# Gate and up tiles of the second block's feed-forward parts as seven half-size products, down tiles dealt out behind them

## The chip, the cores and the metric

The kernel runs on one core of a Trainium2 chip, as one launch. The metric is the device time of that launch in microseconds, the median of three runs. TensorE does the matrix products, VectorE and ScalarE the elementwise work, SyncE (SP) and GpSimd (POOL) issue the DMAs. SBUF is the on-chip memory, PSUM the banks in which TensorE accumulates.

## The reference, cut to what matters

Two blocks of two layers each work on one sequence of 512 tokens and 1024 features, in float32. What the change touches is the second block's feed-forward, which each of its two layers has twice (before and after its mixer), so four times in all:

```python
def swiglu_2(h, w_gu, w_down):
    g, u = jnp.split(h @ w_gu, 2, axis=-1)
    return (jax.nn.silu(g) * u) @ w_down

for l in range(DEPTH):
    h = modulate(rms_norm_2(x, ffn1_norm[l]), mod[0], mod[1])
    x = x + FFN_RESIDUAL * (1 + mod[2])[:, None, :] * swiglu_2(h, ffn1_w_gu[l], ffn1_w_down[l])
    ...
    h = modulate(rms_norm_2(x, ffn2_norm[l]), mod[6], mod[7])
    x = x + FFN_RESIDUAL * (1 + mod[8])[:, None, :] * swiglu_2(h, ffn2_w_gu[l], ffn2_w_down[l])
```

Here h is 512 x 1024, w_gu 1024 x 5632 and w_down 2816 x 1024, and DEPTH is 2. The hidden width of 2816 is 22 tiles of 128 for the gate and 22 for up.

## The kernel before, in words

**Layout and format.** Features lie on the 128 partitions, tokens along the free axis: `xT` is the residual stream, eight slices (KT = 8) of 128 features by 512 tokens. Every matrix product is made of three: a float32 operand z is split into a rounded part `_hi` and the rest `_lo`, both in the fp32r format, and the product is w_hi·h_hi + w_lo·h_hi + w_hi·h_lo. `highs` (L1124) issues the first two (L1127, L1128), `lows` (L1130) the third (L1132). Weights are the stationary operand, 128 by 128, activations the moving one, 512 columns. A gate or up tile (128 hidden features) takes 8 slices x 3 = 24 matmuls.

**A weight tile's way.** SyncE's `load` (L522) fetches 512 KB into one of three places of `raw` once the place is free; ScalarE's `hi` (L674) rounds it into `w_hi` (L678), VectorE's `lo_of` (L1737) writes raw - w_hi into `w_lo` (L1740) and frees the place. TensorE's `tile` (L1141) waits in `slot_ready` for `w_lo` and for the PSUM place of `psP` (three places also) and runs the matmuls. ScalarE's `evac` (L680) copies the bank to `ybuf` (L684). With each tile that it empties, ScalarE rounds the weights of the tile three further on, and VectorE splits them behind its own work on the tile emptied: this order is written out by hand on every engine, and each engine's queue is strictly in order.

**A feed-forward part.** `PARTS` cuts the 22 pairs of gate and up into 8, 7 and 7. For each group, `ffn` runs the pairs, then all 8 down tiles over this group's hidden slices (3 matmuls for each slice), and adds them to `xT`. After a pair VectorE's `gated` (L1859) multiplies SiLU(gate) by up (L1866) and splits the product into `a_hi` (L1869) and `a_lo` (L1870). Each down tile is emptied by ScalarE with the layer's gate as scale, and added by VectorE in `residual` (L1840, add at L1855); with the last group, VectorE also squares and sums `xT` for the next norm (`squares`, L1767), and the eighth tile is added in two halves straight from PSUM (L1851).

**The norm ahead of a part.** TensorE sums the squares over the partitions, VectorE finds the factor (`root`), TensorE spreads it, and VectorE's `scaled` (L1808) writes each slice times gain into one of two places of `tb` (L1824), ScalarE adds the shift and rounds into `h_hi` (L734), VectorE writes `h_lo` (L1818). TensorE starts on the first two tiles (`two_tiles`) as soon as the first slice is there.

**Engines.** SyncE issues all of these loads. POOL has nothing to do in the second block but seven small copies in each layer (L663). The parts are F2 (before the mixer) and F3 (after it), for l = 0 and 1.

## Time and profile before

| | |
|---|---|
| median of 3 runs | 3531.23 us (3527.92 to 3532.91) |
| span of the profiled execution, first to last instruction | 3529.6 us |
| instructions | 45935 |
| TensorE busy | 3498.3 us, 99%, 17160 matmuls |
| VectorE busy | 2067.0 us, 59% |
| ScalarE busy | 1307.9 us, 37% |
| DMA | 387.35 MB, mean 110 GB/s |

The span comes from one profiled execution, and lies 1.6 us below the median of the timed runs. In the rows below, a group reads: line, engine, operation, output <- inputs by name, shapes, how often | busy us, mean ns of one | idle us of the engine just before, and what ended it. PE is TensorE's matmuls, PEld its weight loads, DVE VectorE, ACT ScalarE. A stage's row gives its length, then for PE, PEld, DVE, ACT and POOL the busy time with the number of instructions, then the granted TensorE clock (1.00 is full speed), the share of time the DMA engines were busy, and GB/s. A row in order of time gives start and length in us; "x8" is eight of the same merged.

### The profile page before, as it was taken

To read this page: it belongs to the slowest core of one execution; us is meant where nothing else is said; L and a number is where in the kernel's file an instruction comes from. 1 tells how busy PE (TensorE), PEld (TensorE's weight loads), DVE (VectorE), ACT (ScalarE), POOL (GpSimd) and SP (SyncE) were. 2 spreads that over 40 slices of the span, in tenths; PEclk is the share of its full clock that TensorE was granted. 3 is DMA by queue.
4 is the path that set the end of the run, shared out by engine and by line. 5 is a ranking of instruction groups with operands and counts; after the bars stand their busy time and mean duration, and the time that the engine had idled before them with its cause. 6 is when DMAs were issued, how large, how long until landed. Compare 5 with 4: busy or idle time off the path is not lost.

```text
span 3529.6 us, 45935 instructions
## 1 busy us (share of the span) xinstructions
PE 3498.3 (99%) x17160; PEld 2837.1 (80%) x17160; DVE 2067.0 (59%) x3447; ACT 1307.9 (37%) x2145; POOL 63.8 (2%) x122
## 2 busy tenths in 40 slices
PE   9999999999999999999999999999999999999999
PEld 7777777888876788888888887888888887878887
DVE  5777776666876566685334767433443347673334
ACT  5555554222343332333323444323332234442222
POOL 0000000000000000000000000000000000000000
PEclk9999999999999999999999999999999999999999
DMA  4222223656421365652232212323323322223232
GB/s 145 85 65 78 76 65 106 216 200 206 168 71 49 108 200 194 206 187 94 96 95 93 80 66 73 103 99 96 95 90 97 99 91 77 72 73 100 94 101 79
DMA packets 142102, 387.35 MB, mean 110 GB/s; under 512 B 21680, under 2 KB 63024, under 8 KB 141936
## 3 DMA queue, kind: packets, MB, share of 16 engines
q1 hardware_dynamic: 127024, 306.65, 27.1%
q0 software_dynamic: 14912, 78.52, 6.5%
q8 instruction: 100, 1.64, 0.2%
q14 instruction: 66, 0.54, 0.0%
HBM read 382.11 MB, written 2.10 MB: 109 GB/s over the span
## 4 chain that ended last, share of the span: by engine, by line
PE 95%; DVE 3%; issue 1%; ACT 1%; DMA 0%; SPq 0%; DVEq 0%; ACTq 0%
PE psP L1127 26%; PE psP L1132 25%; PE psP L1128 25%; PE psP L1278 3%; PE psP L1285 3%; PE psP L1279 3%; PE psS L1624 1%; PE psM L1647 1%; PE psS L1341 1%; PE psS L1507 1%; PE psS L1310 1%; PE psS L1323 0%; PE psS L1491 0%; PE psS L1329 0%; PE psS L1635 0%
## 5 line engine op out<-in xcount | busy, mean ns | idle before, releaser
L1127 PE MATMUL psP<-h_hi,w_hi 128*128 128x512 f32 x2664 | 1052.5, 395 | 4.8 <-ACT h_hi L734 2.3
L1128 PE MATMUL psP<-h_hi,w_lo 128*128 128x512 f32 x2664 | 1037.7, 390 | 0.0
L1132 PE MATMUL psP<-h_lo,w_hi 128*128 128x512 f32 x2664 | 1027.8, 390 | 0.0
L1740 DVE TENSOR_TENSOR w_lo<-raw,w_hi 128x1024 fp32r<-128x1024 f32 (+1 forms) x456 | 546.7, 1199 | 396.5 <-ACT w_hi L678 390.4
L684 ACT ACTIVATE ybuf<-psP 128x512 f32<-128x512 f32 (+1 forms) x401 | 239.4, 597 | 1199.5 <-PE psP L1132 1198.1
L1127 PEld LDWEIGHTS psP<-h_hi,w_hi 128*128 128x128 f32 x2664 | 500.5, 188 | 127.2 <-issue 25.8
L1132 PEld LDWEIGHTS psP<-h_lo,w_hi 128*128 128x128 f32 x2664 | 498.3, 188 | 107.7 <-DVE h_lo L1818 4.2
L1128 PEld LDWEIGHTS psP<-h_hi,w_lo 128*128 128x128 f32 x2664 | 500.8, 188 | 99.4
L678 ACT ACTIVATE w_hi<-raw 128x1024 fp32r<-128x1024 f32 (+1 forms) x456 | 471.0, 1033 | 65.4 <-PE psP L1132 65.4
L1127 PE MATMUL psP<-a_hi,w_hi 128*128 128x512 f32 x1248 | 486.3, 390 | 1.2 <-ACT a_hi L1080 1.2
L1128 PE MATMUL psP<-a_hi,w_lo 128*128 128x512 f32 x1248 | 485.6, 389 | 0.0
L1132 PE MATMUL psP<-a_lo,w_hi 128*128 128x512 f32 x1248 | 482.1, 390 | 0.0
L1866 DVE TENSOR_TENSOR prod<-ybuf 128x512 f32<-128x512 f32 x132 | 91.3, 692 | 390.0 <-ACT ybuf L684 343.2
L1855 DVE TENSOR_TENSOR xT<-xT,ybuf 128x512 f32<-128x512 f32 x166 | 114.5, 690 | 279.5 <-ACT ybuf L684 279.5
L1127 PEld LDWEIGHTS psP<-a_hi,w_hi 128*128 128x128 f32 x1248 | 234.2, 188 | 52.3 <-ACT a_hi L1080 2.0
L1132 PEld LDWEIGHTS psP<-a_lo,w_hi 128*128 128x128 f32 x1248 | 233.9, 188 | 49.1 <-DVE a_lo L2521 0.9
L1128 PEld LDWEIGHTS psP<-a_hi,w_lo 128*128 128x128 f32 x1248 | 234.3, 188 | 48.1
L684 ACT ACTIVATE ybuf<-psP,gate 128x512 f32<-128x512 f32 x106 | 72.9, 688 | 314.7 <-PE psP L1132 314.7
L1931 DVE SCALAR_TENSOR_TENSOR ada_acc<-adaw,cact,ada_acc 128x1536 f32<-128x1536 f32 x84 | 152.4, 1814 | 3.4
L1278 PE MATMUL psP<-w_more_hi,a_hi 128*128 128x512 f32 x264 | 109.4, 414 | 0.0
L1285 PE MATMUL psP<-w_more_hi,a_lo 128*128 128x512 f32 x264 | 104.5, 396 | 0.0
L1279 PE MATMUL psP<-w_more_lo,a_hi 128*128 128x512 f32 x264 | 104.4, 395 | 0.0
(336 smaller groups left out, 3545.9 us busy)
## 6 DMA issues: line engine op xcount, KB each, us to landing
raw<-in_gu SPq DMA_DIRECT2D x264, 512.0 KB, 3.3
adaw<-in_ada POOLq DMA_DIRECT2D x96, 768.0 KB, 5.7
raw<-in_down SPq DMA_DIRECT2D x96, 448.0 KB, 3.3
raw<-in_down SPq DMA_DIRECT2D x48, 512.0 KB, 3.6
raw<-in_qkv SPq DMA_DIRECT2D x40, 512.0 KB, 3.6
raw<-in_mix_in SPq DMA_DIRECT2D x34, 512.0 KB, 3.2
raw<-in_qkv SPq DMA_DIRECT2D x64, 256.0 KB, 3.1
raw<-in_wo SPq DMA_DIRECT2D x32, 512.0 KB, 3.3
```

The costliest lines, as they stand in the source:

```text
L678: nc.scalar.activation(w_hi[:, s, 0:cols], raw[:, s, 0:cols], copy).then_inc(hi_done, 1)
L684: nc.scalar.activation(ybuf[0:m, s, :], psP[0:m, s, :], func, **kw).then_inc(evac_done, 1)
L1127: nc.tensor.matmul(psP[:, s, :], hi, rhs[0](kt), start=(n == 0), stop=False)
L1128: nc.tensor.matmul(psP[:, s, :], lo, rhs[0](kt), start=False, stop=False)
L1132: mm = nc.tensor.matmul(psP[:, s, :], w_hi[:, s, kt * P:kt * P + P], rhs[1](kt), start=False, stop=(n == K - 1))
L1278: nc.tensor.matmul(psP[:, m % RING, :], tokens, hi, start=(kt == 0), stop=False)
L1279: nc.tensor.matmul(psP[:, m % RING, :], tokens, lo, start=False, stop=False)
L1285: mm = nc.tensor.matmul(psP[:, m % RING, :], src[1](kt)[:, r * P:(r + 1) * P], hi, start=False, stop=(kt == KT - 1))
L1740: v.tensor_tensor(w_lo[:, s, 0:cols], raw[:, s, 0:cols], w_hi[:, s, 0:cols].bitcast(F32), ALU.subtract)\
L1855: used(v.tensor_tensor(xT[:, m, :], xT[:, m, :], y(), ALU.add), wait=N is not None)
L1866: used(v.tensor_tensor(prod[:, :], g, up, ALU.mult), 2)
L1931: i = v.scalar_tensor_tensor(total, w, at, total, ALU.mult, ALU.add)
```

## The change

All of it lies in F2 and F3. The other parts of the kernel are as before.

- Three of the 22 pairs stay plain tiles. For the other 19, the pair is seen as one product of 2 x 2 blocks: gate and up by the two halves of the 1024 features (weights, blocks of 128 x 512), and the two halves of the features by the early and the late 256 tokens. `product` forms it as seven products of block sums (Winograd's form of Strassen's scheme), each 4 slices x 3 matmuls of 256 columns, in the order P1, P5, P6, P3, P7, P2, P4, accumulated in three PSUM banks (A, E, B).
- Sums of tokens: four combinations of the normed slices (`token_sums`), once for each part, split into `ht_hi` and `ht_lo` (`token_highs` on ScalarE, `token_lows` on VectorE), ahead of and between the first two plain pairs. For them the norm keeps its unshifted slices (`normed_at`) in place of the two places of `tb`.
- Sums of weights, for each pair: SyncE loads five blocks of 256 KB into `s_raw` (A11, S1, S3, A12, A22, with A22 in A11's place), POOL adds a second block onto S1 and onto S3 with an accumulating DMA (`weight_sums`), VectorE forms S2 = A11 + S1 and S4 = A12 + S2. ScalarE rounds and VectorE splits them in four groups (G2: S2, S4; G1: A11, S1; G3: S3, A12; G4: A22).
- Between the products ScalarE copies bank A or E to `st_c` (after P1, P5, P6, P7); TensorE waits for such a copy before it goes on in the same bank. VectorE joins the parts, ScalarE takes SiLU, VectorE gates, ScalarE writes `a_hi`, VectorE `a_lo`.
- Down tiles: six groups of pairs (3, 4, 4, 4, 3, 4) in place of three. A group's eight down tiles are dealt out behind the pairs of the next group, two behind each (3, 3, 2 where that group has three), and the last group's eight stand at the end. VectorE adds each straight from PSUM with the gate (`added`); ScalarE no longer empties them.

```diff
+SEVEN_PARTS = ((0, 3), (3, 4), (7, 4), (11, 4), (15, 3), (18, 4))
+PRODUCTS = (("A", A11, "b11"), ("E", S1, "t1"), ("A", S2, "t2"), ("E", S4, "b22"), ("A", S3, "t3"), ("B", A12, "b21"), ("A", A22, "t4"))
...
@@ sync: ffn_seven @@
+                def load_s1(q):
+                    if q < PAIRS:
+                        if F.pair(l, q):
+                            sp.wait_ge(*s_low.at(low(q - 1, G1)))
+                        sp.dma_start(s_raw[:, S1, :], up_of(q)[:, 0:T]).then_inc(s_landed["s1"].sem, 16)
...
+                for q, (_, _, tiles) in enumerate(frames):
+                    load_a11(q + 1)
+                    load_a22(q + 1)
+                    load_s1(q + 2)
+                    down_load()
+                    load_s3_a12(q + 2)
+                    for _ in tiles[1:]:
+                        down_load()
...
@@ gpsimd: weight_sums @@
+                for q in range(PAIRS):
+                    tile = l * 2 * FT + 2 * (PLAIN + q)
+                    pool.wait_ge(*s_landed["s1"].at(16 * (F.pair(l, q) + 1)))
+                    pool.dma_start(s_raw[:, S1, :], F.gu[tile + 1][:, T:2 * T], accum_op=ALU.add).then_inc(s1_added.sem, 16)
+                    pool.wait_ge(*s_landed["s3"].at(16 * (F.pair(l, q) + 1)))
+                    pool.dma_start(s_raw[:, S3, :], F.gu[tile][:, 0:T], accum_op=ALU.add).then_inc(s3_added.sem, 16)
...
@@ scalar: ffn_seven, for each pair @@
+                    copied(q, P1, "A", C1)
+                    highs_4(q)
+                    copied(q, P5, "E", C5)
+                    copied(q, P6, "A", C2)
+                    copied(q, P7, "A", C3)
+                    if more:
+                        highs_2(q + 1)
+                    act.wait_ge(*s_joined.at(3 * F.pair(l, q) + 3))
+                    nc.scalar.activation(st_c[:, q % 2, C1:C1 + 2, :], st_c[:, q % 2, C1:C1 + 2, :], ACT.Silu).then_inc(s_silu.sem, 1)
+                    if more:
+                        highs_1(q + 1)
+                    act.wait_ge(*s_gated.at(2 * F.pair(l, q) + 2))
...
+                    if more:
+                        highs_3(q + 1)
+                    for _ in tiles:
+                        pos.step()
+                        ahead()
...
@@ tensor: ffn_seven @@
+                def product(p):
+                    name, slot, src = PRODUCTS[p - 1]
+                    fresh = p in (P1, P5, P2)
+                    for k in range(HK):
+                        hi, lo = s_hi[:, slot, k * P:k * P + P], s_lo[:, slot, k * P:k * P + P]
+                        high, low = moving[src](h_hi, ht_hi, k), moving[src](h_lo, ht_lo, k)
+                        start, stop = fresh and k == 0, k == HK - 1
+                        nc.tensor.matmul(bank[name], hi, high, start=start, stop=False, skip_group_check=True)
+                        nc.tensor.matmul(bank[name], lo, high, start=False, stop=False, skip_group_check=True)
+                        mm = nc.tensor.matmul(bank[name], hi, low, start=False, stop=stop, skip_group_check=True)
+                    mm.then_inc(s_product.sem, 1)
...
+                    pe.wait_ge(*s_low.at(4 * pair + G1))
+                    if q:
+                        pe.wait_ge(*s_gated.at(2 * pair))
+                    product(P1)
+                    if q == 0:
+                        pe.wait_ge(t_low, 2 * HK * (F.turn(l) + 1))
+                    product(P5)
+                    pe.wait_ge(*s_copied.at(4 * pair + 1))
+                    product(P6)
+                    pe.wait_ge(*s_copied.at(4 * pair + 2))
+                    product(P3)
+                    pe.wait_ge(*s_low.at(4 * pair + G3))
+                    pe.wait_ge(*s_copied.at(4 * pair + 3))
+                    product(P7)
+                    product(P2)
+                    pe.wait_ge(*s_low.at(4 * pair + G4))
+                    pe.wait_ge(*s_copied.at(4 * pair + 4))
+                    product(P4)
+                    for d, m in tiles:
...
+                        down(d)
...
@@ vector: ffn_seven @@
+                token_sums(0)
+                token_sums(1)
+                token_lows(0)
+                token_lows(1)
+                plain_pair(0)
+                token_sums(2)
+                token_sums(3)
+                token_lows(2)
+                token_lows(3)
+                plain_pair(1)
+                sum_2(0)
+                sum_4(0)
+                lows(0, G2, S2, 2)
+                lows(0, G1, A11, 2)
+                lows(0, G3, S3, 2)
+                plain_pair(2)
+                for q, (n, f, tiles) in enumerate(frames):
+                    more = q + 1 < PAIRS
+                    lows(q, G4, A22, 1)
+                    gate_late(q)
+                    if more:
+                        sum_2(q + 1)
+                    up_late(q)
+                    if more:
+                        sum_4(q + 1)
+                    gate_early(q)
+                    if more:
+                        lows(q + 1, G2, S2, 2)
+                    activated(q)
+                    if more:
+                        lows(q + 1, G1, A11, 2)
+                    a_low(q, n, f)
+                    if more:
+                        lows(q + 1, G3, S3, 2)
+                    for _, m in tiles:
+                        added(m)
+                        ahead()
```

Here `sum_2` and `sum_4` wait for the landings and for POOL's sum on S1, `gate_late` for P3, `up_late` for the copy of P7, `gate_early` for P2, `activated` for the SiLU and for P4; each `highs_n` of ScalarE waits for its inputs and for the product that last read its place; `ahead` prepares the weights of the down tile three further on.

## Rows read from the trace of the kernel before

**Rows 1.** The page: its first line, and busy time by engine.

```profile
span 3529.6 us, 45935 instructions
PE 3498.3 (99%) x17160; PEld 2837.1 (80%) x17160; DVE 2067.0 (59%) x3447; ACT 1307.9 (37%) x2145; POOL 63.8 (2%) x122
```

**Rows 2.** The page's chain that ended last, by engine.

```profile
PE 95%; DVE 3%; issue 1%; ACT 1%; DMA 0%; SPq 0%; DVEq 0%; ACTq 0%
```

**Rows 3.** By stage: block 2's first part, then one of block 1.

```profile
1600.20:1959.20 359.00, 359.00 (x1586) 296.54 (x1584) 154.46 (x199) 112.53 (x144) 0.00 (x0) 1.00 0.30 95
...
600.00:962.00 362.00, 361.41 (x1596) 298.76 (x1597) 256.38 (x261) 111.17 (x146) 24.40 (x45) 1.00 0.59 201
```

**Rows 4.** Costliest groups within 1600.2 to 1959.2 us, each shape by itself.

```profile
L1127 PE MATMUL psP<-h_hi,w_hi 128*128 128x512 f32 x351 | 136.6, 389 | 0.0
...
L1127 PEld LDWEIGHTS psP<-h_hi,w_hi 128*128 128x128 f32 x350 | 65.7, 188 | 13.8
...
L1740 DVE TENSOR_TENSOR w_lo<-raw,w_hi 128x1024 fp32r<-128x1024 f32 x53 | 64.9, 1225 | 65.4 <-ACT w_hi L678 65.4
L678 ACT ACTIVATE w_hi<-raw 128x1024 fp32r<-128x1024 f32 x53 | 55.8, 1052 | 0.0
...
L684 ACT ACTIVATE ybuf<-psP 128x512 f32<-128x512 f32 x44 | 26.3, 599 | 155.8 <-PE psP L1132 155.7
...
L1870 DVE TENSOR_TENSOR a_lo<-prod,a_hi 128x512 f32 x18 | 12.5, 692 | 2.7 <-DVE a_hi L1869 0.7
L1869 DVE CAST a_hi<-prod 128x512 f32 x18 | 7.6, 420 | 0.0
```

**Rows 5.** Short matmuls: order of time (start, length), then one stretch.

```profile
1003.91 1.05 PE L1472 MATMUL psS<-qd,kd 128*128 128x128 f32 x8
1004.80 0.27 PE L1477 MATMUL psS<-ident,ke 128*128 128x128 f32 x1
...
1025.12 0.19 PEld L1127 LDWEIGHTS psP<-h_hi,w_hi 128*128 128x128 f32 x1 [0.38 <-issue]
1025.23 0.19 PEld L1128 LDWEIGHTS psP<-h_hi,w_lo 128*128 128x128 f32 x1
...
543.05:552.80 9.75, 9.66 (x122) 6.60 (x120) 5.54 (x22) 4.39 (x11) 0.00 (x0) 1.00 0.17 55
```

**Rows 6.** Groups of the whole span: shapes nearest to the new ones.

```profile
L1824 DVE SCALAR_TENSOR_TENSOR tb<-xT,gs,psS 128x512 f32<-128x512 f32 x48 | 35.4, 747 | 5.6 <-PE psS L1194 4.0
...
L2229 DVE SCALAR_TENSOR_TENSOR state<-state,decay,psS 128x256 f32<-128x256 f32 x48 | 20.8, 475 | 10.5 <-PE psS L1491 10.5
...
L2063 DVE TENSOR_TENSOR rot<-rot,rot 128x256 f32<-128x256 f32 x32 | 13.6, 425 | 1.1
...
L2362 DVE TENSOR_TENSOR w_lo<-raw,w_hi 128x384 fp32r<-128x384 f32 x16 | 8.9, 555 | 0.2
...
L844 ACT ACTIVATE qk<-psS 128x256 f32<-128x256 f32 x32 | 12.1, 380 | 18.9 <-PE psS L1310 18.9
```

**Rows 7.** DMA issues: size, and median us from issue to landing.

```profile
raw<-in_gu SPq DMA_DIRECT2D x264, 512.0 KB, 3.3
adaw<-in_ada POOLq DMA_DIRECT2D x96, 768.0 KB, 5.7
...
raw<-in_uq SPq DMA_DIRECT2D x16, 192.0 KB, 2.3
...
xT<-in_x POOLq DMA_DIRECT2D x8, 256.0 KB, 3.0
```

**Rows 8.** In order of time: the first part's beginning, TensorE, then VectorE.

```profile
1599.45 0.47 PE L1127 MATMUL psP<-h_hi,w_hi 128*128 128x512 f32 x1 [0.61 <-ACT h_hi L734]
...
1609.56 0.68 DVE L1747 TENSOR_TENSOR w_lo<-raw,w_hi 128x512 fp32r<-128x512 f32 x1
```

**Rows 9.** In order of time: the first part's end, VectorE.

```profile
1957.17 1.22 DVE L1740 TENSOR_TENSOR w_lo<-raw,w_hi 128x1024 fp32r<-128x1024 f32 x1
...
1959.14 0.88 DVE L1851 SCALAR_TENSOR_TENSOR xT<-psP,gate,xT 128x256 f32<-128x256 f32 x2 [0.75 <-PE psP L1132]
```

More of the change, by code:

```diff
@@ L33 @@
 PARTS = ((0, 8), (8, 7), (15, 7))
+SEVEN_PARTS = ((0, 3), (3, 4), (7, 4), (11, 4), (15, 3), (18, 4))
+PLAIN = SEVEN_PARTS[0][1]
+PAIRS = FT - PLAIN
+HK, HT = 4, T // 2
+A11, S1, S2, S4, S3, A12 = range(6)
+A22 = A11
+PRODUCTS = (("A", A11, "b11"), ("E", S1, "t1"), ("A", S2, "t2"), ("E", S4, "b22"), ("A", S3, "t3"), ("B", A12, "b21"), ("A", A22, "t4"))
+P1, P5, P6, P3, P7, P2, P4 = range(1, 8)
+G2, G1, G3, G4 = range(1, 5)
+C1, C2, C3, C5 = 0, 1, 2, 3
 RING = 3
@@ L87, in kt_of, with seven_frames, a_place @@
     return 3 if kind == "q" else KT
+def seven_frames():
+    frames = []
+    for n, (f0, nf) in enumerate(SEVEN_PARTS[1:]):
+        for j in range(nf):
+            first, end = -(-KT * j // nf), -(-KT * (j + 1) // nf)
+            frames.append((n + 1, f0 + j, [(n, m) for m in range(first, end)]))
+    return frames
+def a_place(n):
+    return n % 2 * HK
 def step_units(n):
@@ L458, in __init__, with turn, pair @@
                 self.a_ready = sem(name + "_a_ready")
+            def turn(self, l):
+                return 2 * l + (1 if self is F3 else 0)
+            def pair(self, l, q):
+                return self.turn(l) * PAIRS + q
         ada_landed = [sem(f"ada_landed{i}") for i in range(ADA_RING)]
@@ L723, in hi_half, with norm @@
                     i.then_inc(hi_done, 1)
[L725 removed]
+            def norm(N, l, dst, sh=None, kept=None):
                 hi_half(0)
@@ L1239, in ffn, with ffn_seven, down @@
                             tile(nf, a_split, before=a_wait if m == 0 else None, beside=beside)
+            def ffn_seven(F, l):
+                bank = {"A": psS[:, 0, T:T + HT], "E": psS[:, 1, 0:HT], "B": psS[:, 1, T:T + HT]}
+                early, late = slice(0, HT), slice(HT, T)
+                moving = {"b11": lambda z, t, k: z[:, k, early], "b21": lambda z, t, k: z[:, HK + k, early],
+                          "b22": lambda z, t, k: z[:, HK + k, late], "t1": lambda z, t, k: t[:, k, 0, :],
+                          "t3": lambda z, t, k: t[:, k, 1, :], "t2": lambda z, t, k: t[:, k, 2, :], "t4": lambda z, t, k: t[:, k, 3, :]}
+                def product(p):
[9 more added lines that the diff above has]
+                    mm.then_inc(s_product.sem, 1)
+                def down(n):
+                    nf, at = SEVEN_PARTS[n][1], a_place(n)
+                    tile(nf, ((lambda kt: a_hi[:, at + kt, :]), (lambda kt: a_lo[:, at + kt, :])))
+                two_tiles(KT, h_split, h_wait(F.norm, l))
+                for _ in range(2 * PLAIN - 2):
+                    tile(KT, h_split)
+                a_waited = -1
+                for q, (n, f, tiles) in enumerate(seven_frames()):
+                    pair = F.pair(l, q)
+                    pe.wait_ge(*s_low.at(4 * pair + G1))
+                    if q:
+                        pe.wait_ge(*s_gated.at(2 * pair))
[15 more added lines that the diff above has]
+                    for d, m in tiles:
+                        if d > a_waited:
+                            pe.wait_ge(F.a_ready, l * FT + sum(SEVEN_PARTS[d]) + 1)
+                            a_waited = d
+                        down(d)
+                pe.wait_ge(F.a_ready, l * FT + FT + 1)
+                for m in range(KT):
+                    down(len(SEVEN_PARTS) - 1)
```

270 lines of the change are left out of this document (249 added, 21 removed).

## The prediction

> **What bounds the kernel now.** I read the page's busy times first: TensorE is busy for 99% of the span, VectorE 59%, ScalarE 37% [rows 1]. The chain that ended last says the same from the other side, 95% of it is TensorE [rows 2]. The table by stage then shows the four feed-forward parts of the second block, each a stretch of 359.0 us in which TensorE never stops: 1584 matmuls of 512 columns (44 gate and up tiles of 24, then 8 down tiles of 66), at a granted clock of 1.00 and with DMA at 0.30 of its time or less [rows 3] (the first stretch stands there; the other three have 359.0 too). 359.0 / 1584 = 0.2266 us from one matmul to the next. The single rows give 0.389 us to a matmul and 0.188 us to its weight load [rows 4]; they overlap, so neither is a price. The spacing is. Everything else in these stretches has room: what counts is the number of matmuls, the spacing of each kind, and what can make TensorE wait.
>
> **What the change does to TensorE.** Three of 22 pairs stay plain: 6 x 24 = 144 matmuls, 144 x 0.2266 = 32.6 us. The other 19 pairs went through 48 matmuls of 512 columns, 10.88 us. They become seven products of 4 x 3 = 12 matmuls, 84 of 256 columns. In columns that is 21504 for 24576, one eighth less; in matmuls it is 36 more, and each brings a weight load of its own. Down stays 528 matmuls, 119.6 us, only cut into 48 tiles in place of 24.
>
> So the spacing s of a 256-column matmul with its own 128-column load decides, and the trace has none in this number format. The bounds: [rows 5] show eight 128-column matmuls of full fp32, each with a 128-column load of its own, in 0.89 us, 0.111 each: loads can follow each other that closely while short matmuls run. Where a stretch begins, the second load starts 0.11 after the first [rows 5], so 0.11 is also what a load of our format holds the array up. Half of today's spacing is 0.113. The granted clock of 1.00 is the 2.4 GHz level, where 512 columns are 0.2133 us; if the 0.0133 above that belongs to each matmul and not to each column, s = 0.1067 + 0.0133 = 0.120. The far end is 0.188, a weight load's whole length. I take **0.117**, between 0.113 and 0.120, which are the rows of the same format. Then 19 x 84 x 0.117 = 186.7 us for 206.7: a part falls from 359.0 to 338.9, and four parts save 80 us.
>
> A rule gives more. The Trainium skill, "TensorE: Matmul & The Clock Gate", section "Back-to-back issue gap", puts a warm matmul's gap at its columns over 2.4 GHz plus 2.5 ns. By it s would be 0.109, estimated from that page, and the sum some 50 us lower. The trace disagrees at 512 columns, where it shows 0.2266 and the page says about 0.216.
>
> **Issue.** 84 loads and 84 matmuls in 9.8 us are one instruction per 0.058 us. The densest stretch of the attention ran 122 matmuls and 120 loads in 9.75 us, 0.040 each [rows 5], so issue does not bind at 0.117.
>
> **VectorE at the head of each part.** Its queue is in order. Today TensorE begins at 1599.45 and VectorE ends the norm at 1610.24, 10.8 us later [rows 8]; after it there is slack. Now the four token sums and their splits come first: per slice one add of 0.425, three of 0.475, two splits of 0.69 [rows 4, 6], 3.2 us, 13.0 for four. Two gated pairs with four weight splits add 7.9, the two weight sums 1.4, two splits of two planes 2.5. A gated pair is 0.69 for the product, 0.42 and 0.69 for its two parts [rows 4]. That is 24.8, so 35.6 after the beginning; one wait for ScalarE's rounding (1.05 [rows 4]) and some 20 links of 0.07 make it 38.1. TensorE has only 32.6 us of plain tiles. It loses **5.5 us** a part, the first 2 to 3 of them before tile 3, whose weight split now stands behind the sums; 22 us in all. The lower end is nothing, if the queue packs better; the upper is 8 a part.
>
> **VectorE at the tail.** The last eight down tiles have 12 matmuls, 2.72 us each, where they had 21 (4.76). VectorE has to add the tile (0.75 [rows 6]), square, add (0.69 each) and split the next weights (0.69, or 1.23 for the last three), 2.9 to 3.4 us. Today it ends its last split and then idles 0.75 us before the final residual [rows 9], which follows TensorE's last matmul. Now it falls behind by 0.2 to 0.7 a tile, from a start behind TensorE (the last pair's a_lo is done only 2.6 us after P4), and reaches that residual about 2.2 us late. Three parts have weights to prepare there: **6.6 us**. Before, ScalarE emptied these banks (0.6 to 0.7 us each) beside TensorE; that costs nothing either way.
>
> **Inside the 19 pairs.** VectorE has per pair splits of 0.69 + 3 x 1.23 [rows 4], three joins of 0.425 and two gatings of 0.475, two weight sums and a_lo of 0.69, and for each of two down tiles an add of 0.75 and a split (0.555 [rows 6] to 0.69): 11.4 us. ScalarE has four copies of 0.38 [rows 6], three roundings of 1.05, and rounding, SiLU and a_hi of 0.6 [rows 4] with two more for the down tiles: 7.6. A frame (a pair with the down tiles behind it) on TensorE is 9.83 us of products and 4.1 (8 frames), 5.4 (9) or 8.2 (2) of down tiles: 13.9, 15.3 or 18.0. Both engines fit. The copies that TensorE waits for (P1's before P6, P5's before P3, and so on) have a product of 1.4 us between them and need 0.38 [rows 6] and a hop. The wait before P1 of the next pair has the down tiles as cover: rounding 1.05, split 1.23, after P4. If that cover went, it would cost 2.4 a pair. I book 2 us a part for slips, **8 us**.
>
> **Queues and loads.** A pair now fetches 7 blocks of 256 KB in place of two of 512 KB. SyncE issues five and POOL two, which add onto what landed. Traffic rises from 95 GB/s to about 180; a part of the first block ran at 201 with TensorE busy throughout (the second of [rows 3]), so the volume costs nothing. The order can: SyncE waits for the split of A11 and S1 before it refills S1, POOL waits for that landing, VectorE for POOL's. This is a closed circle once per pair: refill 3.1 us (between 2.3 for 192 KB and 3.3 for 512 KB [rows 7], and the second in the queue), the accumulating transfer x, then sum 0.69, join 0.43, sum 0.69, rounding 1.05, SiLU 0.6, rounding 1.05, split 1.23 and ten hops of 0.07: **9.5 + x**. No row shows an accumulating transfer. A plain one of 256 KB from POOL takes 3.0, one of 768 KB 5.7 [rows 7]. I take 4, nearest to the equal size, since it also has to read what it adds to. 13.5 is under the shortest frame; hidden.
>
> **Sum.** 80.3 - 22 - 6.6 - 8 = 43.7 us off. The profiled execution has a span of 3529.6 us, 1.6 below the median of 3531.2. 3531.2 - 43.7 = **3488 us**.
>
> **Rivals.**
> *The circle binds (slower).* POOL's accumulating transfer takes 6.5 us, more than plain 768 KB. The circle is 16.0; 8 frames lose 2.1 and 9 lose 0.7, 23 us a part, 92 in all: 3580. It decides from x = 5.8 on, where the saving is gone. For it: read, add and write in one transfer, and the whole queue behind it in order. Against it: 3.0 for the same bytes. 16%.
> *The weight load binds (slower).* s = 0.188: 0.071 x 6384 = 453 more, 3941. Against it: [rows 5] have loads of the same kind 0.11 apart. 4%. The Trainium skill, "Perfetto Trace Analysis", section "Identifying the Most-Contended Engine", tells the reader to judge TensorE by the busy share of its weight loads; 84 of 0.188 in 9.8 us would be over 100%, so by that rule this rival is the forecast. The trace speaks against it, as said.
> *The saving drowns (no change).* s = 0.124, where 43.7 / 6384 has been given back: 3531. That is 0.017 above the pure columns in place of today's 0.0133, which would be so if loads and columns hinder each other and now overlap all the time. 10%.
> *Cleaner (faster).* s = 0.111, the row of the fp32 matmuls: 38 us less, 3450. 10%.
> The forecast has 60%, with its own range from 3460 to 3520: s from 0.113 to 0.120, head from 3 to 8 us. That the change does not do what it says is no rival: the matmul counts stand in the code.
>
> **Numbers.** 0.2%, 7 us, is about what a measurement of this kernel can tell. Faster: forecast, cleaner, 70%. Slower: the circle, the load and a part of the third, 21%. Same: 9%. The range from 3435 to 3585 takes in all but the load and the ends of the others.
>
> **What would show it.** Right: 84 matmuls of 256 columns about 0.117 apart; a part of 348 us; TensorE idle some 5 us between the sixth tile and the first product, released by VectorE's split of s_lo or w_lo; POOL's transfers landing under 5 us. Wrong: gaps before P1 in every pair, with the split of A11 and S1 as releaser and s_raw's transfer behind it (the circle); a spacing near 0.19 (the load); or waits between products, which would say that ScalarE's copies come late.

## The result, and the profile after

The changed kernel takes **3662.1 us** (median of 4 runs, 3657.4 to 3668.8) against 3529.6 (3527.9 to 3532.9) on the same chip: 1.038 times the time before, 95% interval 1.036 to 1.039. Forecast were 3488, with a range to 3585. It is slower, and by more than the range allowed. The profiled execution has a span of 3655.7 us; all that follows is read in it.

The page's head, busy times and chain, which answer to [rows 1] and [rows 2]:

```profile
span 3655.7 us, 51647 instructions
PE 3500.2 (96%) x19896; PEld 2951.4 (81%) x19896; DVE 2449.6 (67%) x4275; ACT 1506.2 (41%) x2633; POOL 195.6 (5%) x274
PE 55%; DVE 22%; DMA 15%; ACT 4%; issue 2%; SPq 1%; DVEq 0%; ACTq 0%
DMA s_raw<-in_gu 15%; PE psP L1373 12%; PE psP L1374 12%; PE psP L1378 12%; DVE s_lo L2334 7%; PE psP L1582 3%; PE psP L1589 3%; PE psP L1583 3%; DVE w_lo L2044 2%; ACT s_hi L936 2%; DVE xT L2372 2%; DVE s_raw L2329 1%; DVE s_raw L2323 1%; DVE a_lo L2366 1%; PE psS L1928 1%
```

TensorE was 95% of the chain that ended last; now it is 55%. Its place went to VectorE (22%) and to transfers (15%), and the line names one kind: blocks of gate and up weights on their way into `s_raw`. TensorE's busy time of 3500.2 us is within 2 us of that of before, although the products of 19 pairs in each part have an eighth fewer columns: busy time alone tells neither of the saving nor of the loss.

The table by stage, the first feed-forward part of block two from its first plain matmul to its last down matmul, answers to [rows 3]; under it what TensorE waited for:

```profile
1598.12:1988.75 390.63, 359.33 (x2267) 325.41 (x2268) 248.62 (x402) 162.94 (x267) 32.76 (x38) 0.97 0.48 125
```

```profile
PE psS L1503 <- DVE s_lo L2334: 108.7, 61, 4.6
PE psP L1373 <- DVE w_lo L2044: 11.1, 4, 3.8
```

A part takes 390.6 us (then 390.6, 388.3, 388.2) where it took 359.0 and 348 was forecast. In 61 of 76 pairs TensorE stands before P1 until VectorE has split A11 and S1 (L2334), 108.7 us in all, up to 4.6 at once (counted by the profile as idle time). That is the pattern which the prediction named as the sign of the circle.

Behind the split stand the transfers. The page's rows of DMA issues (number, size, median us from issue to landing), to [rows 7]:

```profile
s_raw<-in_gu SPq DMA_DIRECT2D x380, 256.0 KB, 3.9
adaw<-in_ada POOLq DMA_DIRECT2D x96, 768.0 KB, 6.0
raw<-in_gu SPq DMA_DIRECT2D x112, 512.0 KB, 3.7
s_raw<-in_gu POOLq DMA_DIRECT2D x152, 256.0 KB, 6.3
```

POOL's adding transfers take 6.3 us. By line they divide: those onto S1 (L793) 3.8 at least, 6.6 in the median, 7.8 at most; onto S3 (L795) 3.8, 5.9, 7.5. The fastest agree with the 4 us of the prediction. So the price of adding is not the finding; the question is what makes it 6.6.

One turn of the circle in order of time, SyncE's issues, POOL's and VectorE's (start us, us, engine line, what):

```profile
1773.85 0.33 SPq L666 DMA_DIRECT2D s_raw<-in_gu  x1
1774.23 1.26 SPq L648 DMA_DIRECT2D s_raw<-in_gu  x1
1776.86 0.33 SPq L593 DMA_DIRECT2D raw<-in_down  x1
1777.23 0.43 SPq L660 DMA_DIRECT2D s_raw<-in_gu  x1
1777.70 0.43 SPq L661 DMA_DIRECT2D s_raw<-in_gu  x1
1778.18 0.43 SPq L593 DMA_DIRECT2D raw<-in_down  x1
1778.72 0.37 SPq L654 DMA_DIRECT2D s_raw<-in_gu  x1
```

```profile
1778.42 0.86 POOL L793 DMA_DIRECT2D s_raw<-in_gu  x1 [12.03 <-DMA s_raw<-in_gu]
```

```profile
1772.61 1.22 DVE L2334 TENSOR_TENSOR s_lo<-s_raw,s_hi 128x1024 fp32r<-128x1024 f32 x1
...
1785.43 0.69 DVE L2323 TENSOR_TENSOR s_raw<-s_raw 128x512 f32<-128x512 f32 x1 [5.08 <-DMA s_raw<-in_gu]
...
1790.00 1.22 DVE L2334 TENSOR_TENSOR s_lo<-s_raw,s_hi 128x1024 fp32r<-128x1024 f32 x1
```

The split of A11 and S1 begins at 1772.61. It frees the places: SyncE asks for A22, then for S1 (1774.23). POOL adds to S1 at 1778.42, 4.2 later. VectorE can form S2 at 1785.43, 7.0 later, after an idle 5.1. The next split begins at 1790.00. The circle is 17.4 us: 6.2 of work (6.4 forecast), 4.2 for the refill (3.1) and 7.0 for the addition (4). And POOL's transfer at 1778.42 falls among five transfers which SyncE starts within 2 us: behind two down tiles, S3 and A12, and just ahead of A11 (1778.72).

This turn is one of the slower refills: over all turns the medians are 3.5 us from SyncE's issue of S1 to POOL's, 7.6 from there to S2, and 6.2 for the rest. And S1 is not the only block that S2 = A11 + S1 waits for. What VectorE's sum (L2323) waited for, in us and times, stands under the line that issues each transfer, first SyncE's load of A11 (L654), then POOL's addition onto S1 (L793):

```profile
  DVE s_raw L2323: 256.8, 55
DMA to landing us min/median/max: 3.2/6.4/8.6
```

```profile
  DVE s_raw L2323: 70.7, 17
DMA to landing us min/median/max: 3.8/6.6/7.8
```

In 55 of its 72 waits VectorE's sum was released by A11, the last transfer of the burst, which lands 1.1 us behind S1 there (median). In the turn shown the two land 0.2 us apart. A11 lies on a closed path of its own, which the prediction does not have: the split of A11 and S1 frees A11's place for A22 (issued at 1773.85), A22's split (1778.01) frees it for A11 (1778.72), A11 lands 6.4 later, and then come the sums and the next split. So two closed paths of nearly the same length pass through the same burst. By S1's path alone a turn would take 3.5 + 6.6 + 6.2 = 16.3 us, an estimate from these medians; that too is over the frames of 14.19 and 15.55 us that TensorE needs by itself.

**What a gap costs twice.** From the start of the last matmul before it to the start of P1 it is 0.24 us where nothing is waited for. Summed over the 76 pairs the excess over that is 117.7 us. The seven products take 10.05 us at their usual pace; their excess adds up to another 42.5, 38 of it in 23 pairs with 11.5 to 12.5 us. The table by stage, of the gap of 2.83 us before a pair, of that pair from P1 on, and of the next pair, which had no gap:

```profile
1753.90:1756.70 2.80, 0.43 (x2) 0.01 (x1) 2.80 (x5) 2.30 (x4) 0.00 (x0) 1.00 0.00 0
1756.78:1760.38 3.60, 3.60 (x17) 3.60 (x18) 3.60 (x6) 2.04 (x5) 0.00 (x0) 0.53 0.48 146
1773.90:1777.50 3.60, 3.60 (x31) 3.60 (x31) 3.60 (x6) 2.33 (x5) 0.00 (x0) 1.00 0.48 147
```

In the same 3.6 us 17 matmuls start and 30 start; the granted clock is 0.53, about the 1.2 GHz level, against 1.00. In the gap itself it is still 1.00: here it falls only as TensorE starts again, and the gap of 2.83 us costs another 1.6. Not every gap does. Of the 28 pairs behind a gap of 2.4 us or more 21 had such a stretch at the lower clock, 35 us of the 42.5; of the other 48 none had. The two slow pairs that are left waited 1.05 us each for a copy of ScalarE's between products.

### The profile page after: what moved, and what is told of

Same layout as the page of the kernel before. It is cut to its first block, busy times and chain, and to the rows that moved or that the text cites. A ratio compares the mean times of both kernels' runs of the same rounds, so it can differ in the third digit from the quotient of the medians.

```text
span 3655.7 us, 51647 instructions
## 1 busy us (share of the span) xinstructions
PE 3500.2 (96%) x19896; PEld 2951.4 (81%) x19896; DVE 2449.6 (67%) x4275; ACT 1506.2 (41%) x2633; POOL 195.6 (5%) x274
## 4 chain that ended last, share of the span: by engine, by line
PE 55%; DVE 22%; DMA 15%; ACT 4%; issue 2%; SPq 1%; DVEq 0%; ACTq 0%
DMA s_raw<-in_gu 15%; PE psP L1373 12%; PE psP L1374 12%; PE psP L1378 12%; DVE s_lo L2334 7%; PE psP L1582 3%; PE psP L1589 3%; PE psP L1583 3%; DVE w_lo L2044 2%; ACT s_hi L936 2%; DVE xT L2372 2%; DVE s_raw L2329 1%; DVE s_raw L2323 1%; DVE a_lo L2366 1%; PE psS L1928 1%
## 5 line engine op out<-in xcount | busy, mean ns | idle before, releaser
L1373 PE MATMUL psP<-h_hi,w_hi 128*128 128x512 f32 x1448 | 582.3, 402 | 15.8 <-DVE w_lo L2044 11.1
L1374 PE MATMUL psP<-h_hi,w_lo 128*128 128x512 f32 x1448 | 567.0, 392 | 0.0
L1378 PE MATMUL psP<-h_lo,w_hi 128*128 128x512 f32 x1448 | 557.3, 393 | 0.0
L936 ACT ACTIVATE s_hi<-s_raw 128x1024 fp32r<-128x1024 f32 (+1 forms) x304 | 286.3, 944 | 400.1 <-DVE s_raw L2329 363.8
L2044 DVE TENSOR_TENSOR w_lo<-raw,w_hi 128x1024 fp32r<-128x1024 f32 (+3 forms) x400 | 373.0, 933 | 105.5 <-ACT w_hi L817 102.1
L1503 PE MATMUL psS<-h_hi,s_hi 128*128 128x256 f32 x912 | 268.7, 295 | 110.8 <-DVE s_lo L2334 108.7
L817 ACT ACTIVATE w_hi<-raw 128x1024 fp32r<-128x1024 f32 (+3 forms) x400 | 321.4, 821 | 128.1 <-PE psP L1378 127.8
L2334 DVE TENSOR_TENSOR s_lo<-s_raw,s_hi 128x1024 fp32r<-128x1024 f32 (+1 forms) x304 | 329.7, 1087 | 65.7 <-ACT s_hi L936 65.7
L1503 PE MATMUL psS<-ht_hi,s_hi 128*128 128x256 f32 x1216 | 353.5, 291 | 0.0
L1504 PE MATMUL psS<-ht_hi,s_lo 128*128 128x256 f32 x1216 | 352.9, 290 | 0.0
L1505 PE MATMUL psS<-ht_lo,s_hi 128*128 128x256 f32 x1216 | 352.0, 289 | 0.0
```

The costliest lines, as they stand in the source:

```text
L817: nc.scalar.activation(w_hi[:, s, 0:cols], raw[:, s, 0:cols], copy).then_inc(hi_done, 1)
L936: nc.scalar.activation(s_hi[:, first:first + n, :], s_raw[:, first:first + n, :], copy).then_inc(s_high.sem, 1)
L1373: nc.tensor.matmul(psP[:, s, :], hi, rhs[0](kt), start=(n == 0), stop=False)
L1374: nc.tensor.matmul(psP[:, s, :], lo, rhs[0](kt), start=False, stop=False)
L1378: mm = nc.tensor.matmul(psP[:, s, :], w_hi[:, s, kt * P:kt * P + P], rhs[1](kt), start=False, stop=(n == K - 1))
L1503: nc.tensor.matmul(bank[name], hi, high, start=start, stop=False, skip_group_check=True)
```

## The experiments

Two theories stood at first: **circle** (the closed path through the place of S1) and **traffic** (for each pair 1.75 times the gate and up bytes of before, beside running engines). In the first three kernels the computation is cut, as the expectations say.

### Overwriting in place of adding

```diff
-pool.dma_start(s_raw[:, S1, :], F.gu[tile + 1][:, T:2 * T], accum_op=ALU.add)
+pool.dma_start(s_raw[:, S1, :], F.gu[tile + 1][:, T:2 * T])
```

and the same for S3.

> The changed kernel, but POOL's two transfers of each pair overwrite S1 and S3 in place of adding to them; so the sums A21 + A22 and A11 + A21 are left out of the computation. Everything else, waits and bytes from HBM included, stays. Theory C (circle): a pair's period of 17.5 us is the closed circle split of S1 -> refill of S1 (4.2 us) -> POOL's accumulating transfer (7.0) -> sums, roundings and splits (6.3). A plain transfer of 256 KB from POOL lands in 3.0 to 4 us, the circle falls to about 14.3, at or under TensorE's own 14.1 to 15.5, and the time falls by 130 to 160 us to 3500 to 3525. Theory T (traffic): the period comes from 7 x 256 KB a pair on the DMA queues; the bytes stay, so 3630 to 3660. Theory V (VectorE): its queue of 11 us of work with waits in between sets the period; nothing of it changes, 3640 to 3660.

Measured: 3605.6 us, 1.021 (1.019 to 1.023). Between both theories. POOL's transfer onto S1 still took 5.5 us in the median (3.1 at least), although plain ones of its size took 3.0 in block 1 [rows 7]. Adding costs about 1.1 us; the other 2.5 are something that a plain transfer meets too. The kernel gains only 57 us: A11 still takes 6.0 us in the median, and it is what VectorE's sum waits for in 67 of 71 waits.

### No transfers by POOL

The lines `weight_sums(...)` go, and the two engines wait for SyncE's landings instead.

> The changed kernel without POOL's transfers in the second block's parts: who waited for them waits for SyncE's landing of the same block. The two sums with a second block are left out of the computation. Theory C: the circle is 4.2 + 6.3 = 10.5 us, far under TensorE's work; what is left of the loss is the head and the tail of each part: 3490 to 3505. Theory T: traffic falls from 7 to 5 blocks, so a part of the loss goes, 3560 to 3600. Theory V: 3640 to 3660.

Measured: 3515.4 us, 0.996 (0.994 to 0.997). The x of the circle is gone and with it nearly the whole loss. A11, a transfer of SyncE, gains by it as well: it lands in 4.4 us where it took 6.4. The 10 us over the expectation stand as gaps of 15.7 us before P1 in all.

### One set of weights for a part

SyncE, POOL, ScalarE and VectorE do a part's weight work for its first pair only; 18 pairs reuse it.

> The changed kernel with one set of summed weights for all 19 pairs of a part: from the second pair on nothing is loaded, summed, rounded or split for the products, and P4 uses A11 for A22. So the weights of 18 pairs are left out. TensorE runs the same 84 matmuls of 256 columns a pair, and VectorE and ScalarE still join, gate and add. This is TensorE's floor. Theory C: as without POOL's transfers, within 10 us, so 3485 to 3505, with the 256-column matmuls 0.120 us apart. Theory V: clearly below the kernel without POOL's transfers, by over 50 us. If spacing comes from SBUF traffic of the weights' handling, it falls from 0.120 towards 0.113, and the time by up to 40 us more.

Measured: 3495.8 us, 0.990 (0.988 to 0.992). No gap before P1 in any pair, products of 10.05 us, frames of 14.19, 15.55 and 18.27. The spacing stays at 0.120 with next to none of the weights' handling beside it, so that handling is not what sets it. This is the floor of the scheme with this head and tail. Its span is 160.6 us under that of the changed kernel, and 117.7 + 42.5 from the section above are 160.2: gaps before P1 and the slower products behind them, most of it clock, are the whole difference.

### S1 by itself

S1 is rounded and split alone, right behind the first weight sum, and refilled ahead of A22. All is computed.

```diff
-G2, G1, G3, G4 = range(1, 5)
+GS, G2, G1, G3, G4 = range(1, 6)
...
+                    load_s1(q + 2)
                     load_a22(q + 1)
-                    load_s1(q + 2)
...
                        sum_2(q + 1)
+                        lows(q + 1, GS, S1, 1)
...
-                    highs_of(A11, 2)
+                    highs_of(A11, 1)
```

> The whole computation. S1 is rounded and split by itself right after the sum S2 that reads it, not together with A11 at the end of the pair, and SyncE refills it then, ahead of A22. One more instruction on ScalarE and on VectorE a pair. Theory C: the circle through S1 becomes 4.2 + 7.0 + sum 0.7 + split 0.7 and hops, about 13 us; the next circle (A22, rounding, split, A11, sums, roundings, split) is 13 to 14; TensorE's frames of 14.1 to 15.5 set the period: 3495 to 3530, faster than the changed kernel by 130 us or more and at or below the kernel before. Theory T and theory V: no gain, 3650 to 3670, since bytes and work are the same.

Measured: 3549.7 us, 1.006 (1.004 to 1.008). 112 of the 160 us are back, fewer than expected. The adding transfer onto S1 now takes 4.2 us in the median: it starts long before SyncE's burst. A11 gains too, 4.4 us for 6.4, now that POOL's transfer onto S1 no longer runs beside it. What is left is the other circle, the one through A11's place: VectorE's sum waits for A11 in all its 72 waits. SyncE's queue and VectorE's in this kernel, at one of the longest turns:

```profile
1776.16 0.33 SPq L666 DMA_DIRECT2D s_raw<-in_gu  x1
...
1782.92 0.33 SPq L654 DMA_DIRECT2D s_raw<-in_gu  x1
```

```profile
1775.45 0.68 DVE L2342 TENSOR_TENSOR s_lo<-s_raw,s_hi 128x512 fp32r<-128x512 f32 x1
...
1782.20 0.69 DVE L2342 TENSOR_TENSOR s_lo<-s_raw,s_hi 128x512 fp32r<-128x512 f32 x1 [1.27 <-ACT s_hi L936]
...
1788.21 0.69 DVE L2331 TENSOR_TENSOR s_raw<-s_raw 128x512 f32<-128x512 f32 x1 [3.55 <-DMA s_raw<-in_gu]
...
1793.37 0.68 DVE L2342 TENSOR_TENSOR s_lo<-s_raw,s_hi 128x512 fp32r<-128x512 f32 x1
```

A22 has A11's place. The split of A11 (1775.45) lets SyncE fetch A22 (1776.16); the split of A22 (1782.20) lets it fetch A11 (1782.92); VectorE's sum gets A11 at 1788.21, and the next split of A11 is at 1793.37, 17.9 us after the last.

### Order alone, first try

```diff
-                    load_a11(q + 1)
                     load_a22(q + 1)
                     load_s1(q + 2)
+                    load_a11(q + 2)
+                    if q + 2 < PAIRS:
+                        sp.wait_ge(*s1_added.at(16 * (F.pair(l, q + 2) + 1)))
                     down_load()
```

> The changed kernel with SyncE's order altered and nothing else: A11 of the next pair is fetched right behind S1, and the down tiles, S3 and A12 are asked for only when S1 has been added. All is computed. Theory 'collision' (alone an accumulating transfer takes about 4 us, as predicted; in the changed kernel it starts beside five transfers that SyncE issues within 2 us and so takes 6.6): S1 now lands in 4.0 to 4.6 us, the circle falls from 17.4 to about 15, the gaps before P1 nearly go, 3515 to 3560 us. Rival 'price' (adding in flight costs 6.6 us of itself): S1 still takes over 6 us, the held-back transfers only come later, 3650 us or more.

Measured: 3720.4 us, 1.055 (1.053 to 1.057), the slowest of all. The collision theory was right about the transfer and wrong about the time. The addition onto S1 takes 4.3 us in the median (6.6 in the changed kernel), with little beside it. But A12 stood behind the new wait, and VectorE's second weight sum needs it:

```profile
1787.04 0.69 DVE L2326 TENSOR_TENSOR s_raw<-s_raw 128x512 f32<-128x512 f32 x1 [2.57 <-DMA s_raw<-in_gu]
1787.65 0.42 DVE L2343 TENSOR_TENSOR st_c<-st_c 128x256 f32<-128x256 f32 x1
1791.58 0.69 DVE L2332 TENSOR_TENSOR s_raw<-s_raw 128x512 f32<-128x512 f32 x1 [3.51 <-DMA s_raw<-in_gu]
```

The first sum (L2326) waits 2.6 us, the second (L2332) another 3.5. I had moved a wait ahead of transfers without listing who is behind it.

### More places

`ybuf`, the three places that the plain tiles are emptied to, is idle while products run. It takes A11 and S1 of every second pair, and A22.

```diff
+        def a22_of(q):
+            return ybuf[:, 2, :] if q else s_raw[:, A22, :]
+        def first_of(q):
+            return ybuf if q and q % 2 == 0 else s_raw
...
-                    load_a11(q + 1)
                     load_a22(q + 1)
-                    load_s1(q + 2)
+                    load_s1(q + 3)
+                    load_a11(q + 3)
```

> The changed kernel with more places: A11 and S1 of every second pair go to two idle places of the buffer that empties the plain tiles, A22 to the third, so that A11 and S1 can be fetched a whole pair ahead. All is computed, the traffic is the same. Theory 'circles' (the loss is only the closed circles through the places of A11 and S1; volume and the price of the transfer don't matter once they are open): no gaps before P1, frames of 14.2 / 15.55 / 18.3 us as in the run with one set of weights, 3495 to 3512 us, faster than the kernel before. Rival 'volume' (about 170 GB/s beside running engines slows the matmuls or the transfers): gaps or a spacing over 0.120 stay, 3525 us or more.

Measured: 3501.6 us, 0.992 (0.990 to 0.994): faster than the kernel before. POOL's addition onto S1 takes 5.7 us in the median here and costs nothing, because nobody waits for it: gaps before P1 come to 4.9 us in all 76 pairs. The price of a transfer counts only while it lies on a closed path.

### S1 by itself and A22 in its own place

```diff
-                            sp.wait_ge(*s_low.at(low(q - 1, G4)))
+                            sp.wait_ge(*s_low.at(low(q - 1, G4 if q < 2 else G1)))
                         sp.dma_start(s_raw[:, A11, :], gate_of(q)[:, 0:T])
...
-                        sp.dma_start(s_raw[:, A22, :], up_of(q)[:, T:2 * T])
+                        sp.dma_start(a22_of(q), up_of(q)[:, T:2 * T])
```

> The kernel with S1 handled by itself (3549.7 us) and A22 in a place of its own, so that A11 can be fetched as soon as its own split is done and not behind A22's. All is computed. Theory 'second circle' (what that kernel still loses is A22's fetch, its rounding and split, then A11's fetch, all in one place: 5.4 + 1.4 + 4.9 + 6.2 = 17.9 us in one pair read): 3500 to 3525 us. Rival (what is left is ScalarE's copies, held up behind the rounding of S1: 16.4 us of waits released by st_c): no change, 3540 to 3555.

Measured: 3501.9 us, 0.992 (0.991 to 0.994). The second circle held what was left. The rival is out: ScalarE's order is unchanged, and yet TensorE's waits for its copies fell from 16.4 to 3.0 us. They came with the circle. No run opens A11's path alone and leaves S1's as it was, so how the 160 us divide between the two paths is not shown. The first part in the table by stage, of this kernel and then of the one with a single set of weights:

```profile
1597.00:1947.60 350.60, 346.82 (x2268) 317.84 (x2268) 255.55 (x421) 166.01 (x286) 32.77 (x38) 1.00 0.54 140
```

```profile
1598.50:1948.90 350.40, 346.62 (x2267) 317.85 (x2268) 162.31 (x293) 105.40 (x194) 1.76 (x2) 1.00 0.16 44
```

140 GB/s with the DMA engines busy 0.54 of the time, or 44 with 0.16: 350.6 and 350.4 us. Traffic of this size costs TensorE at most 0.2 us in 350 once nothing waits for it. (The whole kernels lie 6.1 us apart.)

### Order alone, second try

```diff
+                    load_s1(q + 2)
                     load_a22(q + 1)
-                    load_s1(q + 2)
+                    load_a12(q + 2)
+                    load_a11(q + 2)
+                    if q + 2 < PAIRS:
+                        sp.wait_ge(*s1_added.at(16 * (F.pair(l, q + 2) + 1)))
                     down_load()
```

> The changed kernel with SyncE's order altered and nothing else, once more: S1 first, then A22, then A12 and A11 of the next pair, and only the down tiles and S3 wait until S1 has been added (in the order tried before, A12 came behind that wait, and VectorE's second sum of weights waited for it). All is computed. Theory 'collision': S1 lands in 4.3 us and nothing that VectorE's sums need is behind it; the circle is about 15, 3505 to 3535 us. Rival (A11 and A12 beside it slow it as the burst did): S1 takes over 5.5 us, 3580 us or more.

Measured: 3525.0 us (10 runs), 0.9986 (0.9977 to 0.9996). No buffer, no instruction of VectorE or ScalarE is changed, only SyncE's order and one wait in it, and the kernel is 137 us faster than the changed one, of the 160 that gaps and clock had cost. S1 lands in 4.5 us in the median (6.6 before), and A11, which is no longer issued at the end of the burst, in 2.9 (6.4). Two of POOL's additions onto S1:

```profile
1783.26 0.86 POOL L804 DMA_DIRECT2D s_raw<-in_gu  x1 [5.35 <-DMA s_raw<-in_gu]
...
1798.70 0.87 POOL L804 DMA_DIRECT2D s_raw<-in_gu  x1 [5.47 <-DMA s_raw<-in_gu]
```

They stand 15.4 us apart, but that is TensorE's own frame of 15.55, which sets the pace here. Where the frame is 14.19, one P1 follows the other by 14.68 in the median, so the circle is a little under the 15 forecast. That settles the cause: far more the burst than the adding. Without the adding 57 us came back, without the burst 137. What the order does to S1 and what it does to A11 it does together.

### The head

Both kernels start from the one of 3501.9 us.

```diff
+                plain_pair(0)
                 token_sums(0)
                 token_sums(1)
                 token_lows(0)
                 token_lows(1)
-                plain_pair(0)
+                plain_pair(1)
                 token_sums(2)
                 token_sums(3)
                 token_lows(2)
                 token_lows(3)
-                plain_pair(1)
```

This edit, with ScalarE's order to match, is the first kernel.

> The same kernel with three plain pairs as before, only the token sums moved behind the first plain pair. All is computed. Theory 'head': the wait before tile 3 (3.8 us a part) goes, but the sums are then done no earlier and TensorE waits about 4 to 5 us before the first product in its place: 3492 to 3502 us, little or nothing against 3501.9. Rival (each wait is priced by itself): 15 us less, 3487 us.

Measured: 3506.3 us, 0.993 (0.992 to 0.995). The stall moved as expected: the wait before tile 3 is gone, and TensorE waits 16.0 us in four places before the first product instead. The time is 4 us above the expected range; the products that follow these longer gaps run in part at the lower clock (9.3 us over their usual pace in all).

The second has the same edit and one more pair in plain tiles, `SEVEN_PARTS = ((0, 4), (4, 4), (8, 4), (12, 4), (16, 3), (19, 3))`, with `plain_pair(2)` ahead of the first weight sums.

> The kernel in which A22 has a place of its own (3501.9 us), with four plain pairs in place of three, the token sums moved behind the first and the second plain pair on VectorE and ScalarE, and the parts cut 4, 4, 4, 4, 3, 3. All is computed. Theory 'head' (VectorE's queue at the head of each part costs the 6.2 us a part that the changed kernel shows, as the prediction's 5.5): both stalls at the head go, 4 x 6.2 = 25 us, and one pair less by the seven products costs 4 x 0.8 = 3: 3476 to 3486 us. Rival (the stall is set by the norm's and the loads' end, not by the order of VectorE's work): at most the second half goes, 3490 to 3500 us.

Measured: 3500.4 us, 0.992 (0.990 to 0.994), where 3476 to 3486 was expected. Yet both stalls at the head are gone: the first product starts 44.0 us after a part's beginning, and eight plain tiles are 43.5. Who waits now, and VectorE at the end of the part:

```profile
PE psM L1445 <- DVE acc L2095: 11.4, 4, 3.1
```

```profile
1940.31 0.74 DVE L2390 SCALAR_TENSOR_TENSOR xT<-psP,gate,xT 128x512 f32<-128x512 f32 x1
1941.09 0.70 DVE L2094 TENSOR_TENSOR sq<-xT 128x512 f32<-128x512 f32 x1
1941.82 0.69 DVE L2095 TENSOR_TENSOR acc<-acc,sq 128x512 f32<-128x512 f32 x1
1942.55 0.56 DVE L2062 TENSOR_TENSOR w_lo<-raw,w_hi 128x384 fp32r<-128x384 f32 x1
1943.02 0.74 DVE L2390 SCALAR_TENSOR_TENSOR xT<-psP,gate,xT 128x512 f32<-128x512 f32 x1
```

VectorE does not idle in these lines and needs 2.71 us for a tile. I had cut the last group to three hidden slices, so its down tiles have 9 matmuls, 2.04 us. The gain at the head went into the tail: 12.3 us from a part's last down matmul to the next part's first, where the kernel with three plain pairs has 8.2 to 9.8. So one more:

```diff
-SEVEN_PARTS = ((0, 4), (4, 4), (8, 4), (12, 4), (16, 3), (19, 3))
+SEVEN_PARTS = ((0, 4), (4, 4), (8, 3), (11, 3), (14, 4), (18, 4))
```

> The kernel with four plain pairs (3500.4 us), the parts cut 4, 4, 3, 3, 4, 4 in place of 4, 4, 4, 4, 3, 3, so that the last eight down tiles have 12 matmuls (2.72 us) and not 9 (2.04). All is computed. Theory 'tail' (VectorE needs about 2.75 us for each of the last tiles, and with 2.04 us a tile TensorE waited for it: 12.3 us from the last down matmul to the next part where the kernel of three plain pairs had 8.2 to 9.8, and 1.5 us inside the part): the head's 25 us now show, 3480 to 3490 us. Rival (the token sums' new place costs as much as the head gives): no change, 3497 to 3503 us.

Measured: **3481.7 us** (3479.3 to 3482.0) against 3529.0, 0.986 (0.984 to 0.988), all computed: 1.4% faster than the kernel before. The first part of it:

```profile
1597.80:1943.40 345.60, 345.60 (x2232) 316.45 (x2232) 251.29 (x413) 163.09 (x279) 31.04 (x36) 1.00 0.54 139
```

345.6 us of 345.6 busy, at a granted clock of 1.00, and 8.3 to 9.8 us to the next part again. The 25 us that the expectation names are the first part's 6.2 taken four times. In the kernel with three plain pairs (3501.9 us) the four parts lose 6.2, 3.8, 3.8 and 4.8 us before the first product, 18.6 in all, and another 4.5 within their products; less 3 us for the one pair more in plain tiles, that is about the 20 us gained.

## Why the prediction was wrong, step by step

**The step that failed** is "The circle: 9.5 + x, x = 4, 13.5 is under the shortest frame; hidden". Its work was sized right (6.4 forecast, 6.2 measured). Its two transfers were priced as if each ran alone: in the turn shown, refill 3.1 for 4.2 and x 4 for 7.0; in the medians 3.5 and 7.6, so that x is the term that was mis-sized. Of the 7.6, 6.6 are the transfer, and 1.1 more pass until A11 is there too. With little beside it, the addition does take 3.8 to 4.5 us, as the minimum in the changed kernel (3.8) and the medians of four experiments (4.1 to 4.5) show. But the same step that frees S1's place is followed, in SyncE's queue, by five more transfers, and POOL's is issued among them. The prediction had the list of SyncE's orders and the volume, and summed the volume over a pair (180 GB/s, "costs nothing"; by its own block sizes and a part of 348 us it is 142, and 140 was measured with the circles open). The mean was harmless, as the comparison of 350.6 with 350.4 us shows; what the burst does to a transfer on a closed path was not asked.

**A path that was not listed.** A22 has A11's place, so SyncE fetches A11 only behind A22's split. The prediction says "VectorE for POOL's" and stops there; that VectorE's sum waits for A11 as well stood in no term. In 55 of 72 waits it was A11 that came last. The kernel of 3549.7 us, in which S1's path is open and A11's is not, and the one of 3501.9, in which both are, show that this path binds by itself.

**The rival** "the circle binds" had the place and the sign in the profile, and 16%. Its 6.5 us for the transfer is what was measured (6.6), but for another reason: it blamed "read, add and write in one transfer", which is 1.1 us, and not the burst; here it was lucky. Its price was too low as well: 16.0 us a turn for 17.4, 92 us for 160, since it had the refill at 3.1, had no A11 and knew nothing of the clock behind a gap. By its own threshold (the saving is gone from x = 5.8) the measured 6.6 decides.

**Clock.** That TensorE's clock falls behind gaps of this length stood in no term. It made 35 of the 160 us. [rows 3] have 1.00 for stretches in which TensorE never stops, and say nothing of the time behind a gap; the prediction carried the 1.00 over without a word.

**Spacing.** 0.117 taken, 0.120 measured, start to start in order of time:

```profile
1791.61 0.29 PE L1505 MATMUL psS<-h_lo,s_hi 128*128 128x256 f32 x1
1791.73 0.28 PE L1503 MATMUL psS<-h_hi,s_hi 128*128 128x256 f32 x1
1791.85 0.28 PE L1504 MATMUL psS<-h_hi,s_lo 128*128 128x256 f32 x1
1791.97 0.28 PE L1505 MATMUL psS<-h_lo,s_hi 128*128 128x256 f32 x1
```

That is the upper of the two values that bounded it, 0.1067 for the columns and 0.0133 for each matmul, so by these two lengths the overhead belongs to the matmul and not to the column. The seven products take 10.05 us for 9.83, 0.22 x 76 = 17 us less saved. The formula in the Trainium skill ("TensorE: Matmul & The Clock Gate", "Back-to-back issue gap") would have put it at 0.109, an estimate from that page; the trace disagrees here by 0.011, at 512 columns by the same 0.011. The section offers that formula for an isolated matmul, and for a stream of weight loads and matmuls it gives 0.131 us at 512 columns, which is further still from the 0.2266 of this trace.

**Weight load.** The rival of 4% is out. In a pair that ran at a clock of 1.00 throughout, weight loads fill the whole window, and matmuls follow each other at 0.120 all the same:

```profile
1791.27:1801.43 10.16, 10.16 (x85) 10.16 (x85) 5.23 (x8) 3.53 (x8) 1.72 (x2) 1.00 0.74 200
```

A busy share of 100% for the loads does not make them the price: 84 of 0.19 us are 16 us in a window of 10.16, so they overlap. The Trainium skill ("Perfetto Trace Analysis", "Identifying the Most-Contended Engine") judges TensorE's headroom by this share, beside the share of peak arithmetic; the trace agrees that no headroom is left, and disagrees with what the rival made of it, a spacing of 0.188.

**Head.** Right. Forecast was the first product at 38.1 us, measured 38.8, 37.5, 37.5 and 37.5; forecast were "the first 2 to 3 us before tile 3", measured 3.8 in the first part and 2.4 to 2.5 in the others. The first part's:

```profile
1618.81 0.50 PE L1373 MATMUL psP<-h_hi,w_hi 128*128 128x512 f32 x1 [3.78 <-DVE w_lo L2044]
```

In all the head costs 6.2 + 3 x 4.9 = 21 us for 22. The sum behind it holds a slip: two gated pairs with four weight splits are 8.5 us by the prices it names, not 7.9. The experiments on the head show it to be VectorE's queue.

**Tail.** Forecast 2.2 us in three places, 6.6; from the last down matmul to the next part 9.5, 8.3 and 8.9 us measured where it was 6.4, 6.2 and 6.2, 7.9 in all. Right in kind and nearly in size.

**Slips.** The 8 us for them were not used: with one set of weights there was no wait between products at all.

**The sum, mended.** 3488 + 160 (circles and clock) + 17 (spacing) - 8 (slips) + 1 (tail) - 1 (head) gives 3657; measured 3662. With the circles open, 3488 + 17 - 8 + 1 - 1 = 3497; measured 3501.6 and 3501.9. What is left, some 5 us, is not accounted for.

## What to carry to other kernels

Price a transfer on a closed path with what is issued around it, not alone: write down each queue's issues in order of time for one turn, and look at which of them start within the same two microseconds. List every transfer that the next step waits for, not only the one that looks dear: here it was most often the plain load of A11 that came last. Before you price such a circle, ask whether it can be opened: an idle buffer as a second place made the transfer's price irrelevant. And when a stall at one end is covered by giving an engine more time, check the same engine at the other end: the first version with four plain pairs gained nothing because its last tiles were too short for VectorE.

## What the runs showed of the hardware that I had not expected

- An adding transfer of 256 KB issued by POOL lands in 4.1 to 4.5 us (medians of four kernels; 3.7 at least) when little else is under way and in 6.6 (median) amid five others of up to 256 KB; a plain one by POOL at the same spot takes 5.5, and 3.0 in block 1 of the kernel before. Adding costs about 1 us, company 2.1 to 2.5. Its issue holds POOL for 0.86 us.
- A plain load of 256 KB issued by SyncE as the last of the same burst lands in 6.4 us (median), and in 2.9 where it is issued by itself.
- Behind a gap of 2.83 us TensorE's granted clock was 0.53 for the next 3.6 us, and the seven products took 11.63 us in place of 10.05; in the gap itself it was still 1.00. Of 28 pairs behind gaps of 2.4 to 5.0 us, 21 were slow in this way and seven ran at 1.00 throughout.
- 256-column matmuls in fp32r, each with a weight load of 0.19 us of its own, start every 0.120 us over 10 us on end; 512-column ones every 0.227.
